# VectorE takes the next piece of scores ahead of a block's low half in two attention stages

## The chip, the cores and the metric

The kernel runs on one core of a Trainium2 chip, as one launch. The time is device microseconds of a run; three runs of the kernel before give a median of 3399.77 us (3396.58 to 3401.65).

The engines named here: TensorE (PE in the profile, PEld its weight loads), VectorE (DVE), ScalarE (ACT), GpSimd (POOL) and SyncE (SP, which issues DMAs). Each executes its own list of instructions in order, and they wait for each other through semaphores.

## The reference

The program computes two transformer layers on 2048 tokens of width 1024, batch 1, float32.

The first layer has two attentions beside each other. The first ("mla") has 8 heads with queries and keys of 96 values and values of 64, causal, with softmax over all earlier keys:

```python
sc = einsum('bqhd,bkhd->bhqk', qb, k) * scale
p = softmax(where(causal, sc, -inf))
o = einsum('bhqk,bkhd->bqhd', p, v)
```

The second ("dsa") has 8 query heads of 64 values that share 2 heads of keys and values. An index score chooses at most 256 earlier keys for each query, and the softmax runs over these alone. Both outputs are gated, projected, weighed with sigmoids, added and projected again. The second layer is a causal window attention of 128 keys with a bias by distance and sink terms, gated and projected, with a norm at the end. The change touches only the two softmax attentions of the first layer.

## The kernel before

The program is a sequence of stages with a barrier after each: front projections, the mla attention, the index scores with the choice of keys (and the gates' projections), the dsa attention, merge, window attention, final. `stage_attention` (line 906) builds both attention stages from a description of the layer (`Mla`, line 1151, and `Dsa`, line 1717).

**Units.** A stage works through 32 units, numbered 0 to 31. A unit has four rows s of 128 queries each, and a number of key blocks j of 128 keys. In mla a unit is one head and 512 queries; its rows see 128(4g+1) to 128(4g+4) keys, and g runs 0, 1, 2, 3, 3, 2, 1, 0 over the units, again and again. Its last four blocks are the diagonal ones, so block 4g+3 concerns only one row (128 columns). In dsa a unit is one tile t of 128 queries and one of the two key heads; its rows are four query heads, all with 128(t+1) keys. The units are t = 0, 0, 1, 1, ... 15, 15. The choice of keys comes as an additive mask.

**Steps.** `schedule` (line 859) writes one list of steps, which every engine walks, each taking its own part:
- "S": one piece of scores, at most 512 keys of one row. TensorE multiplies (three matmuls in mla, two in dsa) into one of 3 PSUM banks `p_s`. VectorE waits for `scored`, adds the mask into `probs` and takes the maximum of the piece (L1051), and increments `moved`. After a row's last piece it reduces the maxima (L1069) and writes the shift (L1073).
- "E": ScalarE takes exp of the row (L1116), after the shift.
- "B": one key block of a unit. TensorE transposes the exps of up to four rows into one of 3 banks `p_t` (L1021). ScalarE copies it, rounded, to `th`, the high half (L1124, `hi_done`). VectorE subtracts and writes the rest to `tl`, the low half (L1081, `lo_done`). Three blocks later TensorE multiplies both with the values into `p_o` (L985, L987).
- "V": TensorE transposes the inverted sums (L1033), ScalarE copies them (L1131). VectorE has no part in it; it inverts the sums at the unit's block 0 (L1089).
- "O": VectorE multiplies the output with them (L1102).

**The order.** The unit with "S" steps is one ahead of the unit with "B" steps. Each unit begins with a lead of 8 "S" (or all, where there are fewer), then the blocks of the unit before follow, and the rest of the "S" is spread evenly between them. Written with S for a piece, S. for the last piece of a row, e for its exp, B for block 0, b for a later block, the list of unit 28 of mla and that of unit 12 of dsa (with the blocks of units 27 and 11) are

```
SSSS.SeSSS.BSebbOSbbSbbS.bbSebbSbbSbbS.bVe
SS.SeS.SeS.SeS.BbbObbVe
```

**What waits for what.** Before the scores of piece i TensorE waits until piece i-3 is moved (line 1012), before the transposes of a block until the low three uses of `p_t` earlier is done (`wait_bank`, line 995). VectorE waits for `scored` (line 1050) before a piece and for `hi_done` (line 1080) before a low. ScalarE writes a slot of `th` only after the multiplication four blocks earlier.

Of the kernel before, what the change touches and what calls it, by code (L numbers as in the profile page):

```python
# [858 lines left out]
def schedule(units, behind, lead, output_late, batched):  # L859

    steps, late = [], []
    blocks = 0
    for n in range(len(units) + behind):
        m = n - behind
        s_steps = []
        if n < len(units):
            for s in range(4):  # L870
                keys = units[n]["keys"][s]
                for c, k0 in enumerate(range(0, keys, GT)):
                    s_steps.append(("S", n, s, c, k0, min(GT, keys - k0), k0 + GT >= keys))
        b_steps = [("B", m, i, j, s0) for i, (j, s0) in enumerate(units[m]["blocks"])] + [("V", m)] if m >= 0 else []
        pending = []

        def take_scores():
            nonlocal pending
            step = s_steps.pop(0)
            steps.append(step)  # L880
            steps.extend(pending)
            pending = []
            if step[6] and not batched:
                pending = [("E", n, step[2])]
            elif step[6] and step[2] == 3:
                pending = [("E", n, s) for s in range(4)]

        for _ in range(min(lead, len(s_steps))):
            take_scores()
        total, rest = len(b_steps), len(s_steps)  # L890
        for x in range(total):
            steps.append(b_steps[x])
            blocks += steps[-1][0] == "B"
            while late and late[0][1] <= blocks:
                steps.append(("O", late.pop(0)[0]))
            while s_steps and (rest - len(s_steps)) * total < (x + 1) * rest:
                take_scores()
        while s_steps:
            take_scores()
        steps += pending  # L900
        if m >= 0:
            late.append((m, blocks + output_late))
    return steps + [("O", n) for n, _ in late]


def stage_attention(nc, sem, tag, ident, layer, space):


# [3 lines left out]
    R, S = layer.depth, layer.split_ring  # L912
    steps = schedule(units, R - 1, layer.lead, layer.output_late,
                     layer.batched)
    n_b = [sum(len(u["blocks"]) for u in units[:n]) for n in range(len(units) + 1)]
    A = layer.score_banks
    B = 6 - A
    ring = lambda n, place: (n_b[n] + n + place) % B
    n_sub = lambda n, s: 4 * n + s
    with ExitStack() as c:  # L920
# [27 lines left out]
        @block.sync  # L948
        def _(sp):
            ahead = layer.ahead  # L950
            for n in range(ahead):
                layer.load(sp, n)
            for n in range(len(units)):
                if n + ahead < len(units):
                    layer.load(sp, n + ahead)
                if n >= 1:
                    sp.wait_ge(out_done, n)
                    sp.dma_start(layer.store(n - 1), ot[:, (n - 1) % 2]).then_inc(stored[(n - 1) % 2], 16)
                layer.sync_unit(sp, n)
            n = len(units) - 1  # L960
            sp.wait_ge(out_done, n + 1)
            sp.dma_start(layer.store(n), ot[:, n % 2]).then_inc(stored[n % 2], 16)
            for p in range(2):
                sp.wait_ge(stored[p], 16 * len(range(p, len(units), 2)))
            layer.sync_end(sp)
# [73 lines left out]
        @block.vector  # L1039
        def _(dve):  # L1040
            layer.dve_start(dve)
            i = 0
            for step in steps:
                if step[0] == "S":
                    _, n, s, ch, k0, w, last = step
                    if ch == 0:
                        layer.wait_bias(dve, n, s)
                        if n >= R and s == 0:
                            dve.wait_ge(turned, n_b[n - R + 1])
                    dve.wait_ge(scored, i + 1)  # L1050
                    nc.vector.tensor_tensor_reduce(  # L1051
                        out=probs[n % R][:, s, k0:k0 + w], in0=p_s[:, i % A, 0:w],
                        in1=layer.bias(n, s, k0, w), scale=1.0, scalar=layer.least_max(n, s),
                        op0=ALU.add, op1=ALU.max, accum_out=maxes[:, n % R, s, ch:ch + 1]).then_inc(moved, 1)
                    i += 1
                    if layer.batched:
                        if s == 3:
                            if n >= R:
                                dve.wait_ge(exped, n_sub(n - R, 3) + 1)
                            dve.wait_ge(moved, i)  # L1060
                            nc.vector.tensor_scalar(shift[:, n % R], maxes[:, n % R, :, 0], -layer.scale, None,
                                                    ALU.mult).then_inc(shifted, 1)
                            layer.shift_made(dve, n, shift[:, n % R])
                    elif last:
                        m = maxes[:, n % R, s, 0:1]
                        dve.wait_ge(moved, i)
                        if ch > 0:
                            m = top[:, n % R, s:s + 1]
                            nc.vector.tensor_reduce(m, maxes[:, n % R, s, 0:ch + 1], AX.X, ALU.max)  # L1069
                            dve.drain()  # L1070
                        if n >= R:
                            dve.wait_ge(exped, n_sub(n - R, s) + 1)
                        nc.vector.tensor_scalar(shift[:, n % R, s:s + 1], m, -layer.scale, None,  # L1073
                                                ALU.mult).then_inc(shifted, 1)
                elif step[0] == "B":
                    _, n, place, j, s0 = step
                    b = n_b[n] + place
                    if b >= S:
                        dve.wait_ge(multiplied, b - S + 1)
                    dve.wait_ge(hi_done, b + 1)  # L1080
                    nc.vector.tensor_tensor(tl[:, b % S, s0 * P:GT], p_t[:, ring(n, place), s0 * P:GT],  # L1081
                                            th[:, b % S, s0 * P:GT].bitcast(F32),
                                            ALU.subtract).then_inc(lo_done, 1)
                    if place == 0:
                        dve.wait_ge(exped, n_sub(n, 3) + 1)
                        layer.add_sinks(dve, n, sums[:, n % R])
                        if n >= 2:
                            dve.wait_ge(inv_turned, n - 1)
                        nc.vector.reciprocal(inv[:, n % 2], sums[:, n % R]).then_inc(inverted, 1)  # L1089
                elif step[0] == "O":  # L1090
                    n = step[1]
                    dve.wait_ge(multiplied, n_b[n + 1])
                    dve.wait_ge(spread_done, n + 1)
                    if not layer.packed:
                        if n >= 2:
                            dve.wait_ge(stored[n % 2], 16 * (n // 2))
                        nc.vector.tensor_tensor(ot[:, n % 2], p_o[0:HD, n % 2], spread[0:HD, n % 2],
                                                ALU.mult).then_inc(out_done, 1)
                        continue
                    if n >= 2:  # L1100
                        dve.wait_ge(out_done, n - 1)
                    nc.vector.tensor_tensor(halves[:, n % 2], p_o[:, n % 2], spread[:, n % 2],  # L1102
                                            ALU.mult).then_inc(weighed, 1)
# [1874 lines left out]
def program(nc, a, out):  # L2978
    with ExitStack() as c:
# [16 lines left out]
        with ExitStack() as c1:  # L2996
            bias = BiasJob(nc, c1, a["one_hot"], a["t5_table_2"], spread)
            at, end = -(-nc.sbuf_base // 64) * 64, nc.sbuf_usable_end
            rest = Space(nc, (at + 2 * H_HALF, end))
            index_in = IndexInputs(nc, rest, at, qiT, kiT, wi, h_dram, a["w_in"][0],  # L3000
                                   a["b_merge"][0].rearrange("a n -> (a n)"))
            kept = rest.ranges[0][0]
            mla = Mla(nc, qkT, va, oaT, bias, at, kept)
            mla.index_in = index_in
            stage_front(nc, sem, ident, a, h_dram, qkT, qbT, kbT, qiT, kiT, va, vb, wi, bias, mla)
            sem.end_stage()
            stage_attention(nc, sem, "mla", ident, mla, Space(nc, (kept + H_HALF // 4, end)))
            sem.end_stage()
# [72 lines left out]
```

## Time and profile before

| | |
|---|---|
| median of three runs | 3399.77 us |
| profiled execution, its own time | 3407.41 us |
| its span | 3405.6 us |
| granted TensorE clock, mean | 0.965 |
| TensorE busy | 3153.2 us (93%) |
| VectorE busy | 2075.5 us (61%) |
| ScalarE busy | 1823.7 us (54%) |
| mla attention | about 447.6 to 938.7 us of the span |
| dsa attention | about 1617.2 to 2082.1 us |

"Busy" counts from the start of an instruction to its end; instructions of one engine can overlap in the profile, so two that follow without a gap are often less than one duration apart. An idle time in brackets in a timeline is the time before that instruction in which its engine did nothing, and the name behind the arrow is what ended it.

### The profile page before, as it was taken

How to read it: one execution, taken by the hardware profiler on the slowest of the kernel's cores; microseconds unless marked ns; L12 is line 12 of the kernel's file. 1: busy time of each engine (PE TensorE's matmuls, PEld its weight loads, DVE VectorE, ACT ScalarE, POOL GpSimd, SP SyncE). 2: the span in 40 equal slices, each digit the busy share in tenths (PEclk: the TensorE clock that was granted, in tenths of full speed). 3: DMA queues.
4: the chain of work that ended last, by engine and by line, in shares of the span. 5: the costliest groups of instructions: out<-in, count | busy, mean ns of one | idle time of the engine just before them, and what ended most of it. 6: DMA issues, size and time to landing. Idle time of an engine off the chain costs nothing. (4 is left out here: it accounts for less than half of the span.)

```text
span 3405.6 us, 51222 instructions
## 1 busy us (share of the span) xinstructions
PE 3153.2 (93%) x17304; PEld 2648.2 (78%) x17304; DVE 2075.5 (61%) x5122; ACT 1823.7 (54%) x3613; POOL 779.4 (23%) x1078
## 2 busy tenths in 40 slices
PE   6999879999979999996899997899989999969998
PEld 5888768888868777775667776899878888859997
DVE  5767668888845756663899885444446666632112
ACT  5665556667656666663777774211246666632121
POOL 6444411111112122232211101111034444311110
PEclk8999989999989999998899998999999999979999
DMA  4666654436152222235411103444432222144432
GB/s 166 203 199 199 204 132 97 88 69 141 58 196 85 67 88 77 79 91 124 107 42 31 31 19 110 147 133 138 165 135 74 74 65 64 55 143 133 124 124 74
DMA packets 307189, 370.46 MB, mean 109 GB/s; under 512 B 24801, under 2 KB 251937, under 8 KB 303089
## 3 DMA queue, kind: packets, MB, share of 16 engines
q1 hardware_dynamic: 293728, 320.77, 32.5%
q0 software_dynamic: 13200, 46.42, 4.3%
q8 instruction: 139, 2.28, 0.3%
q14 instruction: 122, 0.99, 0.1%
HBM read 216.32 MB, written 150.80 MB: 108 GB/s over the span
## 5 line engine op out<-in xcount | busy, mean ns | idle before, releaser
L93 PE MATMUL i_p_g<-i_hT_lo,i_wh 128*128 128x512 f32 x768 | 308.9, 402 | 9.3 <-DVE i_wl L1632 9.3
L94 PE MATMUL i_p_g<-i_hT_hi,i_wl 128*128 128x512 f32 x768 | 306.7, 399 | 0.0
L95 PE MATMUL i_p_g<-i_hT_hi,i_wh 128*128 128x512 f32 x768 | 306.2, 399 | 0.0
L1650 DVE SCALAR_TENSOR_TENSOR i_score<-i_relu,i_w,i_score 128x1024 f32<-128x1024 f32 (+7 forms) x154 | 155.1, 1024 | 167.9 <-ACT i_relu L1534 166.1
L1544 ACT ACTIVATE i_above<-i_score,i_less 128x2048 bf16<-128x2048 f32 (+13 forms) x140 | 183.2, 1308 | 105.7 <-POOL i_less L1601 69.1
L1081 DVE TENSOR_TENSOR mla_tl<-mla_p_t,mla_th 128x512 fp32r<-128x512 f32 (+1 forms) x320 | 186.2, 606 | 45.2 <-ACT mla_th L1124 41.9
L1124 ACT ACTIVATE mla_th<-mla_p_t 128x512 fp32r<-128x512 f32 (+1 forms) x320 | 164.0, 530 | 86.9 <-PE mla_p_t L1021 84.1
L1081 DVE TENSOR_TENSOR dsa_tl<-dsa_p_t,dsa_th 128x512 fp32r<-128x512 f32 x272 | 180.1, 686 | 42.8 <-ACT dsa_th L1124 37.1
L1051 DVE CUSTOM_DVE_ANT_0 dsa_probs<-dsa_p_s,dsa_mask 128x512 f32<-128x512 f32 (+3 forms) x320 | 184.6, 605 | 26.4 <-PE dsa_p_s L1796 24.7
L1124 ACT ACTIVATE dsa_th<-dsa_p_t 128x512 fp32r<-128x512 f32 x272 | 155.4, 593 | 70.5 <-PE dsa_p_t L1021 69.5
L1534 ACT ACTIVATE i_relu<-i_p_s 128x1024 f32<-128x1024 f32 (+7 forms) x176 | 141.5, 813 | 77.2 <-PE i_p_s L1502 38.6
L1021 PE MATMUL mla_p_t<-ident,mla_probs 128*128 128x128 f32 x1088 | 172.7, 274 | 10.9 <-DVE mla_tl L1081 9.5
L93 PEld LDWEIGHTS i_p_g<-i_hT_lo,i_wh 128*128 128x128 f32 x768 | 146.3, 191 | 45.2 <-issue 10.2
L1116 ACT ACTIVATE dsa_probs<-dsa_probs,dsa_shift 128x128 f32<-128x128 f32 (+15 forms) x128 | 153.9, 1202 | 43.7 <-DVE dsa_shift L1073 43.3
L93 PE MATMUL b_p_p<-b_wl,b_xh 128*128 128x512 f32 (+1 forms) x384 | 161.8, 421 | 14.9 <-DVE b_wl L588 14.9
L1116 ACT ACTIVATE mla_probs<-mla_probs,mla_shift 128x1280 f32<-128x1280 f32 (+15 forms) x128 | 153.6, 1201 | 40.5 <-DVE mla_shift L1073 39.0
L1021 PE MATMUL dsa_p_t<-ident,dsa_probs 128*128 128x128 f32 x1088 | 169.8, 280 | 5.9 <-ACT dsa_probs L1116 2.7
L1795 PE MATMUL dsa_p_s<-dsa_k_hi,dsa_q 128*128 128x512 f32 (+3 forms) x320 | 131.6, 413 | 45.9 <-PEq L70 25.6
L95 PEld LDWEIGHTS i_p_g<-i_hT_hi,i_wh 128*128 128x128 f32 x768 | 146.3, 190 | 35.4
L93 PE MATMUL m_p_b<-m_ol,m_bh 128*128 128x256 f32 x512 | 148.9, 291 | 26.6 <-POOL m_ol L2690 22.3
L1021 PEld LDWEIGHTS dsa_p_t<-ident,dsa_probs 128*128 128x128 f32 x1088 | 134.1, 143 | 50.1 <-DVE dsa_tl L1081 19.7
L94 PEld LDWEIGHTS i_p_g<-i_hT_hi,i_wl 128*128 128x128 f32 x768 | 146.4, 191 | 31.4
(334 smaller groups left out, 9699.4 us busy)
## 6 DMA issues: line engine op xcount, KB each, us to landing
scratch_gates<-i_ob SPq DMA_DIRECT2D x96, 256.0 KB, 2.4
m_m<-scratch_gates SPq DMA_DIRECT2D x64, 256.0 KB, 4.2
f_hs<-scratch_h2T SPq DMA_DIRECT2D x16, 1024.0 KB, 9.8
scratch_qkT<-b_th SPq DMA_DIRECT2D x64, 192.0 KB, 2.6
scratch_qkT<-b_tl SPq DMA_DIRECT2D x64, 192.0 KB, 2.9
i_ws<-in_w_in SPq DMA_DIRECT2D x24, 512.0 KB, 4.6
b_xt<-in_x SPq DMA_DIRECT2D x16, 512.0 KB, 4.9
scratch_h<-b_xh POOLq DMA_DIRECT2D x16, 512.0 KB, 3.0
```

Of the source, the lines that this page charges most:

```text
L93: pe.matmul(out, l[0], r[1], start=start, stop=False)
L94: pe.matmul(out, l[1], r[0], start=False, stop=False)
L95: return pe.matmul(out, l[0], r[0], start=False, stop=stop)
L1021: last = nc.tensor.transpose(p_t[:, ring(n, place), s * P:(s + 1) * P], probs[n % R][:, s, j * P:(j + 1) * P], ident[:])
L1051: nc.vector.tensor_tensor_reduce(out=probs[n % R][:, s, k0:k0 + w], in0=p_s[:, i % A, 0:w], in1=layer.bias(n, s, k0, w), scale=1.0, scalar ...
L1081: nc.vector.tensor_tensor(tl[:, b % S, s0 * P:GT], p_t[:, ring(n, place), s0 * P:GT], th[:, b % S, s0 * P:GT].bitcast(F32), ALU.subtract). ...
L1116: nc.scalar.activation(x, x, ACT.Exp, bias=shift[:, n % R, s:s + 1], scale=layer.scale, accum_out=sums[:, n % R, s:s + 1]).then_inc(exped, 1)
L1124: nc.scalar.activation(th[:, b % S, s0 * P:GT], p_t[:, ring(n, place), s0 * P:GT], ACT.Copy).then_inc(hi_done, 1)
L1534: nc.scalar.activation(relu[:, n % 3, 0:width], p_s[:, n % 2, 0:width], ACT.Relu).then_inc(relued, 1)
L1544: nc.scalar.activation(above[:, 0:keys], score[:, x % 2, 0:keys], ACT.Sign, bias=less[:, x % 2:x % 2 + 1], accum_out=signs[:, i % 2:i % 2 ...
L1650: nc.vector.scalar_tensor_tensor(out=acc, in0=r, scalar=w[:, t, h:h + 1], in1=acc, op0=ALU.mult, op1=ALU.add).then_inc(summed, 1)
L1795: self.nc.tensor.matmul(out, q, self.k_hi[:, g, k0:k0 + w], start=True, stop=False)
```

## The change

VectorE walks a reordered copy of the step list in both attention stages. `scores_ahead` holds back each "B" step except a unit's block 0 until the next "S" has been taken, or until another "B" or an "O" comes. "V" and "E" steps, which VectorE skips, are left out of its list and don't end the holding. The other engines walk the list as before.

```diff
@@ -903,6 +903,24 @@
     return steps + [("O", n) for n, _ in late]
 
 
+def scores_ahead(steps):
+
+
+    order, held = [], []
+    for step in steps:
+        if step[0] == "S":
+            order += [step] + held
+            held = []
+        elif step[0] in "BO":
+            order += held
+            held = [step] if step[0] == "B" and step[2] else []
+            if step[0] == "B" and not step[2]:
+                order.append(step)
+            if step[0] == "O":
+                order.append(step)
+    return order + held
+
+
 def stage_attention(nc, sem, tag, ident, layer, space):
@@ -1040,7 +1058,7 @@
         def _(dve):
             layer.dve_start(dve)
             i = 0
-            for step in steps:
+            for step in scores_ahead(steps):
                 if step[0] == "S":
                     _, n, s, ch, k0, w, last = step
                     if ch == 0:
```

## Rows read from the trace of the kernel before

**Rows 1.** Windows: busy us (and instructions) by engine, clock, DMA, in each stage.
```profile
447.60:938.70 491.10, 476.47 (x2816) 398.18 (x2816) 408.55 (x1247) 339.72 (x609) 58.66 (x64) 0.98 0.42 96
1617.20:2082.10 464.90, 432.89 (x2400) 331.00 (x2400) 403.96 (x1199) 332.23 (x561) 58.58 (x62) 0.97 0.18 43
```
**Rows 2.** Groups by shape, VectorE, mla: xcount | busy, mean ns | idle before, releasers.
```profile
L1081 DVE TENSOR_TENSOR mla_tl<-mla_p_t,mla_th 128x512 fp32r<-128x512 f32 x224 | 148.5, 686 | 43.7 <-ACT mla_th L1124 41.9 <-issue 0.6
...
L1081 DVE TENSOR_TENSOR mla_tl<-mla_p_t,mla_th 128x128 fp32r<-128x128 f32 x32 | 9.2, 286 | 0.3
```
**Rows 3.** Waits in the dsa stage: who <- whom: us in total, times, longest us.
```profile
PEld dsa_p_s L1795 <- DVE dsa_maxes L1051: 58.7, 115, 1.3
ACT dsa_probs L1116 <- DVE dsa_shift L1073: 43.3, 74, 1.2
DVE dsa_tl L1081 <- ACT dsa_th L1124: 37.1, 62, 3.7
...
PEld dsa_p_t L1021 <- DVE dsa_tl L1081: 19.7, 46, 1.0
```
**Rows 4.** Timeline, dsa unit 12: start us, us, instruction [idle before <-releaser].
```profile
1702.21 0.69 DVE L1081 TENSOR_TENSOR dsa_tl<-dsa_p_t,dsa_th 128x512 fp32r<-128x512 f32 x1 [0.21 <-ACT dsa_th L1124]
...
1702.45 0.39 PE L1796 MATMUL dsa_p_s<-dsa_k_lo,dsa_q 128*128 128x512 f32 x1
...
1703.02 0.69 DVE L1051 CUSTOM_DVE_ANT_0 dsa_probs<-dsa_p_s,dsa_mask 128x512 f32<-128x512 f32 x1
...
1703.63 0.56 DVE L1051 CUSTOM_DVE_ANT_0 dsa_probs<-dsa_p_s,dsa_mask 128x384 f32<-128x384 f32 x1
...
1704.25 0.19 PEld L1795 LDWEIGHTS dsa_p_s<-dsa_k_hi,dsa_q 128*128 128x128 f32 x1 [0.18 <-DVE dsa_maxes L1051]
```
**Rows 5.** Timeline, start of dsa unit 22.
```profile
1845.96 0.39 PE L1796 MATMUL dsa_p_s<-dsa_k_lo,dsa_q 128*128 128x512 f32 x1
...
1846.60 0.68 DVE L1051 CUSTOM_DVE_ANT_0 dsa_probs<-dsa_p_s,dsa_mask 128x512 f32<-128x512 f32 x1
```
**Rows 6.** Timeline, end of dsa unit 29, start of unit 30.
```profile
2011.17 0.34 PE L1796 MATMUL dsa_p_s<-dsa_k_lo,dsa_q 128*128 128x384 f32 x1
...
2012.03 0.55 DVE L1051 CUSTOM_DVE_ANT_0 dsa_probs<-dsa_p_s,dsa_mask 128x384 f32<-128x384 f32 x1
...
2013.03 0.69 DVE L1051 CUSTOM_DVE_ANT_0 dsa_probs<-dsa_p_s,dsa_mask 128x512 f32<-128x512 f32 x1
```
**Rows 7.** Timeline, start of mla unit 14.
```profile
668.29 0.39 PE L95 MATMUL mla_p_s<-mla_k_hi,mla_q_hi 96*128 96x512 f32 x1
...
668.83 0.69 DVE L1051 CUSTOM_DVE_ANT_0 mla_probs<-mla_p_s,mla_none 128x512 f32<-128x512 f32 x1 [1.02 <-PE mla_p_s L95]
...
669.58 0.19 PEld L93 LDWEIGHTS mla_p_s<-mla_k_lo,mla_q_hi 96*128 96x128 f32 x1 [0.31 <-DVE mla_maxes L1051]
```
**Rows 8.** Timeline of ScalarE, mla unit 15.
```profile
686.26 0.60 ACT L1116 ACTIVATE mla_probs<-mla_probs,mla_shift 128x384 f32<-128x384 f32 x1
```
**Rows 9.** Timeline, mla unit 13, blocks 12 to 15 of unit 12.
```profile
664.73 0.39 PE L95 MATMUL mla_p_s<-mla_k_hi,mla_q_hi 96*128 96x512 f32 x1
...
665.66 0.68 DVE L1051 CUSTOM_DVE_ANT_0 mla_probs<-mla_p_s,mla_causal 128x512 f32<-128x512 f32 x1
...
666.43 0.27 PE L1021 MATMUL mla_p_t<-ident,mla_probs 128*128 128x128 f32 x1
...
666.73 0.89 DVE L1081 TENSOR_TENSOR mla_tl<-mla_p_t,mla_th 128x384 fp32r<-128x384 f32 x2
```
**Rows 10.** Timeline of weight loads, dsa unit 21.
```profile
1839.86 0.44 PEld L1021 LDWEIGHTS dsa_p_t<-ident,dsa_probs 128*128 128x128 f32 x4 [0.20 <-DVE dsa_tl L1081]
```
**Rows 11.** Timeline, dsa unit 28, blocks 1 and 5 of unit 27.
```profile
1975.22 0.69 DVE L1081 TENSOR_TENSOR dsa_tl<-dsa_p_t,dsa_th 128x512 fp32r<-128x512 f32 x1 [1.29 <-ACT dsa_th L1124]
...
1977.18 0.42 PEld L1021 LDWEIGHTS dsa_p_t<-ident,dsa_probs 128*128 128x128 f32 x4 [0.52 <-DVE dsa_tl L1081]
```

## The prediction

> **What bounds the kernel now.** I read the slice table of the page first, then the busy time of the two attention stages, the waits inside each, and last the timeline of each engine where the new order differs. Both stages are TensorE's: it is busy 476.5 of 491.1 us in the first and 432.9 of 464.9 us in the second [rows 1]. VectorE has 408.6 and 404.0 us of work there, 83% and 87% [rows 1], and is never far from the path, because TensorE runs at most three banks ahead of it on either kind of work. VectorE idles 41.9 us in the first stage before lows, until ScalarE has written the high half [rows 2], and 37.1 us in the second, at 62 places [rows 3]. In the second stage TensorE's weight loads wait 58.7 us for a score bank and 19.7 us, at 46 places, for a low [rows 3]. The reader is to see that VectorE has idle time, and to ask whether it lies where order can use it.
>
> **What the edit does to the order.** Worked out from the step list, it exchanges 98 neighbouring pairs (low, piece of scores) in the first stage and 90 in the second. It adds and removes no instruction, no DMA and no semaphore; all other engines keep their lists. VectorE executes in order, so what moves is a wait: at such a pair it waits for `scored` first, and the low stands behind that wait. Who waits for a low: TensorE, three blocks later. Who waits for a piece: TensorE, three pieces later, and at a row's end ScalarE's exp.
>
> TensorE issues a block's transposes, two multiplications of an older block, then the piece, and ScalarE's copy takes less time than those matmuls. If nobody is behind, the old order is thus the order in which things become ready, and the new one can only win where ScalarE is late with the high half.
>
> **Unit starts, second stage (+9.3).** A "V" step does not release a held low, so the last low of a unit also goes behind the first piece of the next lead. Unit 12: the low runs at 1702.21 while TensorE still computes the piece, whose last matmul ends at 1702.45 + 0.39 = 1702.84; VectorE starts it at 1703.02 (0.18 us after) and the next at 1703.63, so a step costs 0.61 us start to start [rows 4]. New: VectorE idles to 1703.02, takes the piece to 1703.63 and the low to 1704.24; the second piece is 0.61 us late. The lead of eight pieces runs at VectorE's pace: TensorE's load of the fifth waits 0.18 us for the bank of the second [rows 4], so it moves too, and so do the exps, which wait 43.3 us of the stage for shifts [rows 3]. Nothing later in the unit gives this back, since the whole chain moves. Alike are units 10 to 16 and 24: 8 x 0.61 = 4.9 us. In units 8 and 9 VectorE reached the piece a little late, 0.45 each by the same arithmetic, 0.9. Unit 5 has one piece a row, and its exps may cover it: I take 0. In units 17 to 23 VectorE was just behind: in unit 22 the piece's last matmul ends at 1845.96 + 0.39 = 1846.35, so it was ready at 1846.53, and VectorE, in the low until then, took it at 1846.60 [rows 5]. That low began 0.61 us before, at 1845.99. New: idle to 1846.53, pair done at 1847.75 instead of 1847.21, 0.54 late. Seven such, at 0.5: 3.5. Bounds of the term: 0, and 18 x 0.61 = 11.0.
>
> **Unit ends, second stage (+2.0).** In units 25 to 31 the last pair is a low and the short last piece. In unit 29 its second matmul ends at 2011.17 + 0.34 = 2011.51, ready about 2011.69; piece, maximum and shift take 2013.03 - 2012.03 = 1.00 us [rows 6]; with the low behind it, the next unit starts at 2013.30, 0.27 late. The seven give 0.1 to 0.4 each, 2.0 us (bounds 0 and 3).
>
> **First stage (+9.2).** A unit's last low has 128 columns and takes 0.29 us, its end hidden under the next instruction [rows 2], 0.28 start to start. At 668.83 VectorE had waited 1.02 us for the first piece, so the low was free; behind the piece it makes the second 0.28 us late, and TensorE waits for banks here also, 0.31 us at 669.58 [rows 7]. 23 of the units 2 to 31 have more than one piece a row: 6.4 us. Seven have one, and there the exps follow each other without a gap (one at 686.26 with no wait before it) [rows 8], so ScalarE hides the delay; without that cover it would be 7 x 0.28 = 2.0, and I take 0. Bounds 0 and 8.4.
> One inner pair hurts more, in units 5, 13, 21 and 29: the low of block 12 goes behind a row's last piece and its shift. The piece is ready at 664.73 + 0.39 + 0.15 = 665.27 (0.15 as between 668.29 + 0.39 and 668.83 [rows 7]) and takes 666.73 - 665.66 = 1.07 us with its shift; the low then ends at 666.34 + 0.69 = 667.03. TensorE took block 15, which needs that low, at 666.43 [rows 9], and goes on 0.6 to 0.7 us later; the unit's end and the next lead hang on it. 4 x 0.7 = 2.8 us, bounds 0 and 3. The other inner pairs of this stage fall where VectorE is behind anyway or idles next: 0.
>
> **Inner pairs, second stage (-1.1).** Loss: in units 21 to 23 TensorE already waits for the low of block 3 (0.20 us at 1839.86 [rows 10]), which now comes 0.61 later; I count 0.4 each, 1.2 us (0 to 1.8). Gain: in units 24 to 28 VectorE idles 1.1 to 1.3 us before the low of block 1, because ScalarE is in an exp, and the piece behind it is long computed. It now fits into that wait: the low stays at 1975.22, what follows comes 0.61 earlier, and TensorE's wait of 0.52 us at 1977.18 goes [rows 11]. Late next is the high half, so not all of it counts: 5 x 0.45 = 2.3 us (0 to 3.1).
>
> A rule of the Trainium skill, page "Perfetto Trace Analysis", section "Identifying the Most-Contended Engine", is to optimise the engine of highest occupancy first (for TensorE it wants other measures than matmul time). TensorE's busy share is 97% and 93% [rows 1], so by that rule a new order of equal work on VectorE would leave 3400 us. The bank waits of [rows 4, 7] speak against it at unit starts.
>
> **Sum.** 9.3 + 2.0 + 9.2 - 1.1 = 19.4 us slower. The profiled execution took 3407.4 us (span 3405.6), 7.6 above the runs' median of 3399.8; the sum gives 3427 against itself and, carried over, 3419 for the median. Nothing outside the two stages changes.
>
> **Rivals.**
> A. Faster: the piece fills ScalarE's exp waits, the 79 us of [rows 2, 3]. But they must fall on exchanged pairs. Following the timeline, 44 of the 188 pairs have one, 17 us in all, mostly of the size in [rows 4] (0.21); nine are of 0.8 us or more, like that of [rows 11]. If these nine gave 0.6 each and ScalarE covered every unit start, 3399.8 - 5.4 = 3394. It decides from the point where the exps set the pace of a lead; the 43.3 us that ScalarE waits for shifts [rows 3] say that VectorE does. Chance 0.07.
> B. Same: three banks absorb 0.3 to 0.6 us at a unit start, and what is left cancels, 3400 (3393 to 3407). For it: the occupancies [rows 1]. Against: TensorE waits for banks at just these places [rows 4, 7], so the ring is used up there. Chance 0.13.
> C. Slower by more: lows that come 0.61 us or, behind a shift, about 1 us later lengthen the 46 waits for lows of [rows 3]. At 0.2 us each that is 9 us on top: 3428. Against: most of these waits follow a late high half, which the order doesn't move. Chance 0.12.
> D. As summed, perhaps with part of a term hidden: 3410 to 3425. Chance 0.68.
> That the list is not what it seems (a pair not exchanged) would show as B.
>
> 0.2% (6.8 us) is about what a measurement of this kernel can tell from no change. Faster by more: A, 0.07. Within: B, 0.13. Slower: C and D, 0.80. The range takes in D, most of C and the half of B nearest to it: 3398 to 3431.
>
> **What would show it.** In the changed profile the first stage is about 9 us longer and the second about 10. VectorE's waits for `scored` appear at nearly every unit start of the second stage, while its waits for the high half shrink by at most some 10 us a stage. TensorE's waits for score banks in the leads grow, block 15 of units 5, 13, 21 and 29 waits for a low, and the wait of 0.52 us before block 5 in unit 28 is gone. I am wrong if those waits of VectorE appear and the stages keep their length (the ring absorbs them), or if TensorE's waits for banks and lows fall in sum.

## Result and the profile after

Five runs of each: 3416.02 us median (3415.96 to 3417.91) against 3399.77 us (3396.58 to 3402.76). The ratio is 1.0050, 95% interval 1.0040 to 1.0061: slower by 16.3 us by the medians. The profiled execution has a span of 3416.1 us, against 3405.6.

The windows of the two stages in the changed kernel, which answer to [rows 1] (stretch, length, busy us of PE, PEld, DVE, ACT, POOL, clock, DMA share, GB/s):

```profile
446.80:944.90 498.10, 480.27 (x2816) 398.17 (x2816) 409.55 (x1248) 339.52 (x609) 58.57 (x64) 0.98 0.42 94
1622.60:2095.00 472.40, 430.95 (x2400) 329.73 (x2400) 405.41 (x1199) 330.91 (x561) 58.44 (x62) 0.98 0.18 42
```

The first stage is 7.0 us longer (498.1 - 491.1), the second 7.5 (472.4 - 464.9). VectorE's work is the same to 1.5 us. TensorE's busy time is 3.8 us more in the first stage and 1.9 less in the second; its idle time grew by 3.2 and 9.4 us. Between the whole spans of these two profiled executions lie only 10.5 us (3416.1 - 3405.6), because the stages whose code did not change took 4.0 us less in the second of them. The profile before also holds an accident that can be placed: its granted clock was below full speed for part of a 20 us stretch of the second stage, and the two units there (8 and 9) took 10.26 and 11.05 us, where the profiles of inner pairs alone and of block 1 alone (below) show 8.65 and 9.46. The same stretch in the windows of the kernel before and of the changed kernel:

```profile
1660.00:1680.00 20.00, 17.84 (x86) 13.36 (x85) 15.73 (x61) 12.56 (x26) 3.75 (x4) 0.83 0.31 61
```
```profile
1660.00:1680.00 20.00, 16.64 (x91) 11.64 (x89) 17.55 (x62) 14.07 (x31) 5.64 (x6) 1.00 0.28 57
```

The clock was 0.83 in the first and 1.00 in the second. Put right by 1.6 + 1.6 us, the second stage grew by 10.7.

Waits in the second stage after, as in [rows 3] (who <- whom: us in total, times, longest us):

```profile
PEld dsa_p_s L1813 <- DVE dsa_maxes L1069: 66.2, 112, 1.3
ACT dsa_probs L1134 <- DVE dsa_shift L1091: 52.5, 66, 1.6
DVE dsa_probs L1069 <- PE dsa_p_s L1814: 42.4, 36, 21.9
DVE dsa_tl L1099 <- ACT dsa_th L1142: 27.8, 48, 3.0
...
PEld dsa_p_t L1039 <- DVE dsa_tl L1099: 18.6, 41, 1.0
```

The wait of VectorE for pieces in the kernel before:

```profile
DVE dsa_probs L1051 <- PE dsa_p_s L1796: 24.7, 3, 21.8
```

VectorE's wait for the high half fell from 37.1 to 27.8 us. In its place stands a wait for pieces, 36 times instead of 3; the longest, 21.8 us before and 21.9 after, is the start of the stage, so the rest grew from 2.9 to 20.5 us. Behind it TensorE waits longer for banks (58.7 to 66.2) and ScalarE for shifts (43.3 to 52.5). In the first stage the same trade, groups by shape as in [rows 2]; the last line is that of the kernel before for the same pieces:

```profile
L1099 DVE TENSOR_TENSOR mla_tl<-mla_p_t,mla_th 128x512 fp32r<-128x512 f32 x224 | 148.9, 686 | 31.2 <-ACT mla_th L1142 28.9 <-issue 0.6
L1069 DVE CUSTOM_DVE_ANT_0 mla_probs<-mla_p_s,mla_none 128x512 f32<-128x512 f32 x192 | 129.0, 687 | 27.8 <-PE mla_p_s L95 27.2
...
L1051 DVE CUSTOM_DVE_ANT_0 mla_probs<-mla_p_s,mla_none 128x512 f32<-128x512 f32 x192 | 127.8, 686 | 16.1 <-PE mla_p_s L95 15.4
```

The wait for the high half fell from 41.9 to 28.9 us, that for these pieces rose from 15.4 to 27.2.

**A unit start, second stage.** Unit 12 after, the timeline of VectorE and of the weight loads, to be laid beside [rows 4]:

```profile
1708.51 0.69 DVE L1069 CUSTOM_DVE_ANT_0 dsa_probs<-dsa_p_s,dsa_mask 128x512 f32<-128x512 f32 x1 [1.01 <-PE dsa_p_s L1814]
...
1709.13 0.69 DVE L1099 TENSOR_TENSOR dsa_tl<-dsa_p_t,dsa_th 128x512 fp32r<-128x512 f32 x1
1709.73 0.55 DVE L1069 CUSTOM_DVE_ANT_0 dsa_probs<-dsa_p_s,dsa_mask 128x384 f32<-128x384 f32 x1
...
1710.34 0.19 PEld L1813 LDWEIGHTS dsa_p_s<-dsa_k_hi,dsa_q 128*128 128x128 f32 x1 [0.78 <-DVE dsa_maxes L1069]
```

The low, which ran in a gap before, waits through 1.01 us of idle VectorE, and the second piece starts 1.22 us after the first instead of 0.61. The load of the fifth piece, which waited 0.18 us, waits 0.78 (the last line shown). (Unit 11 has six blocks, so the list of unit 12 ends in `BbbObbbVe`, with one b more behind the O than shown ahead; the pair at the unit start is the same.)

**Inside a unit, first stage.** Unit 13 after, to be laid beside [rows 7, 9]:

```profile
667.57 0.69 DVE L1069 CUSTOM_DVE_ANT_0 mla_probs<-mla_p_s,mla_causal 128x512 f32<-128x512 f32 x1 [0.67 <-PE mla_p_s L95]
...
668.64 1.49 DVE L1099 TENSOR_TENSOR mla_tl<-mla_p_t,mla_th 128x512 fp32r<-128x512 f32 x3
671.47 0.69 DVE L1069 CUSTOM_DVE_ANT_0 mla_probs<-mla_p_s,mla_none 128x512 f32<-128x512 f32 x1 [1.35 <-PE mla_p_s L95]
...
672.09 0.28 DVE L1099 TENSOR_TENSOR mla_tl<-mla_p_t,mla_th 128x128 fp32r<-128x128 f32 x1
672.29 0.28 DVE L1069 CUSTOM_DVE_ANT_0 mla_probs<-mla_p_s,mla_causal 128x128 f32<-128x128 f32 x1
...
669.39 0.14 PEld L1039 LDWEIGHTS mla_p_t<-ident,mla_probs 128*128 128x128 f32 x1 [0.81 <-DVE mla_tl L1099]
```

The row's last piece and its shift go first, the low of block 12 only at 668.64, and TensorE waits 0.81 us for it before block 15. At the start of unit 14 VectorE's wait for the first piece grew from 1.02 to 1.35 us, and the low, free before, stands between the first and the second piece.

**The gain.** Unit 28 after, to be laid beside [rows 11]:

```profile
1986.83 0.69 DVE L1069 CUSTOM_DVE_ANT_0 dsa_probs<-dsa_p_s,dsa_mask 128x512 f32<-128x512 f32 x1
...
1988.11 1.29 DVE L1099 TENSOR_TENSOR dsa_tl<-dsa_p_t,dsa_th 128x512 fp32r<-128x512 f32 x2 [0.58 <-ACT dsa_th L1142]
```

The wait for the high half shrank from 1.29 to 0.58 us, because the piece fits into it, and two lows follow each other without a gap. TensorE's wait of 0.52 us before block 5 is gone; at the load behind that one a wait of 0.35 us for a low is new, so not all of it is gained.

### The profile page after: what moved, and what is told of

Same layout as the page of the kernel before. It is cut to its first block and busy times, and to the rows that moved or that the text cites. A ratio compares the mean times of both kernels' runs of the same rounds, so it can differ in the third digit from the quotient of the medians.

```text
span 3416.1 us, 51222 instructions
## 1 busy us (share of the span) xinstructions
PE 3152.4 (92%) x17304; PEld 2644.2 (77%) x17304; DVE 2077.7 (61%) x5122; ACT 1821.2 (53%) x3613; POOL 777.6 (23%) x1078
## 5 line engine op out<-in xcount | busy, mean ns | idle before, releaser
L1099 DVE TENSOR_TENSOR mla_tl<-mla_p_t,mla_th 128x512 fp32r<-128x512 f32 (+1 forms) x320 | 186.5, 605 | 32.6 <-ACT mla_th L1142 28.9
L1099 DVE TENSOR_TENSOR dsa_tl<-dsa_p_t,dsa_th 128x512 fp32r<-128x512 f32 x272 | 179.6, 685 | 31.4 <-ACT dsa_th L1142 27.8
L1134 ACT ACTIVATE dsa_probs<-dsa_probs,dsa_shift 128x128 f32<-128x128 f32 (+15 forms) x128 | 153.8, 1201 | 53.0 <-DVE dsa_shift L1091 52.5
L1039 PEld LDWEIGHTS mla_p_t<-ident,mla_probs 128*128 128x128 f32 x1088 | 133.4, 140 | 50.9 <-DVE mla_tl L1099 21.0
L1039 PEld LDWEIGHTS dsa_p_t<-ident,dsa_probs 128*128 128x128 f32 x1088 | 132.7, 142 | 49.3 <-DVE dsa_tl L1099 18.6
```

The source lines that it names most:

```text
L1039: last = nc.tensor.transpose(p_t[:, ring(n, place), s * P:(s + 1) * P], probs[n % R][:, s, j * P:(j + 1) * P], ident[:])
L1134: nc.scalar.activation(x, x, ACT.Exp, bias=shift[:, n % R, s:s + 1], scale=layer.scale, accum_out=sums[:, n % R, s:s + 1]).then_inc(exped, 1)
```

## Experiments

To place a difference I take from each timeline the moment at which VectorE starts a unit's first piece; the time to the next unit's first piece is the unit's length. Away from the first units of a stage (up to unit 7 in the second) and from disturbed clock, equal code gives equal lengths to 0.04 us, which makes them sharper than the time of a run. One length falls out: unit 26 of the second stage is 0.35 us longer in wait alone, at full granted clock and without an exchanged start, and I have not traced why. Lengths in us:

```
unit                  mla 5   mla 9  mla 13  dsa 12  dsa 21  dsa 25  dsa 30
before                22.17    8.83   22.51   11.29   17.46   20.52   24.06
changed               22.93    9.03   22.95   11.88   18.58   20.08   24.24
starts alone          22.35    9.02   22.67   11.89   18.00   20.52   24.05
inner pairs alone     22.74    8.83   22.75   11.29   18.18   20.08   24.23
block 1 alone         22.15    8.83   22.50   11.29   17.47   20.13   24.05
late V                21.88    8.47   22.12   11.08   17.46   20.51   24.05
changed + late V      22.50    8.59   22.70   11.46   18.16   20.06   24.25
wait alone            22.34    9.01   22.34   11.85   17.94   20.53   24.05
```

Sums of lengths run, if nothing else is said, to the start of unit 31, in the first stage from unit 2 and in the second from unit 5, since no low is exchanged in the units ahead of these. (Those units differ from profile to profile all the same: unit 2 of the second stage is 0.65 us longer in the changed kernel and in inner pairs alone.) Units 8 and 9 of the second stage are compared with those of block 1 alone, because the profile before is disturbed there. Summed in this way the change costs 6.1 us in the first stage and 10.1 in the second, 16.2 us, against 16.3 by the medians.

The diffs show the lines that decide; `late_turn` and `follows_v` are helpers that move the V steps and find the exchanged starts.

**Starts alone.** The exchanges across a V step, no others.

```diff
-            held = [step] if step[0] == "B" and step[2] else []
+            held = [step] if step[0] == "B" and step[2] and steps[x + 1][0] == "V" else []
```

> Only the exchanges across a V step are made (26 in the first stage, 18 in the second): the last low of a unit goes behind the first piece of the next. Readiness theory (at a unit start VectorE idles until the first piece is computed, and the low then delays the second piece): 0.2 us at each start of the first stage, about 4.5 to 5 us, and 0.5 to 0.6 us at each start of the second, about 9.5 us; 3399.8 + 14 = 3414, most of the change's 16 us. Rival (the lows inside the units, which TensorE waits for, carry the loss): at most 4 us, 3404.

3415.86 us against 3401.22 for the kernel before on that chip, ratio 1.0040 (1.0027 to 1.0053). The lengths: 0.2 us in 22 units of the first stage, 4.3 in sum from unit 2 on; 0.42 to 0.62 at each start of the second, 10.0 in sum. For unit 8, disturbed in this profile too (10.29 us), that sum takes the 0.51 us of the changed kernel, which makes the same exchange there. So most of the loss is here.

**Inner pairs alone.** V releases a held low.

```diff
-        elif step[0] in "BO":
+        elif step[0] in "BOV":
             order += held
```

> Only the exchanges inside a unit are made (72 and 72); a V step releases a held low. Readiness theory: units 5, 13, 21, 29 of the first stage +0.25 to 0.55 each (block 15 waits for the low of block 12), 1.6 to 2 us; second stage +0.5 in units 21 to 23, -0.45 in units 24 to 28 and the last-piece pairs of units 25 to 31 a further 1 to 2, so 0 to +1.5; in all +2 to +4, 3403. Rival (inner lows carry the loss): +12 or more, 3412.

3403.83 us, ratio 1.0006 (0.9997 to 1.0015), no change by time. The lengths show what cancels: first stage +0.57 and +0.24 in units 5 and 13, as in 21 and 29, with small ones 2.1 in sum; second stage +0.7 to +0.9 in units 21 to 23 and -0.3 to -0.6 in 24 to 28, +0.5 in sum. By time the rival of this expectation, 12 us or more for the inner lows, is out. In unit 21 the weight load that waited 0.20 us for the low [rows 10] waits 0.61 more:

```profile
1836.74 0.20 PEld L1036 LDWEIGHTS dsa_p_t<-ident,dsa_probs 128*128 128x128 f32 x2 [0.81 <-DVE dsa_tl L1096]
```

Starts and inner pairs together are 4.3 + 2.1 and 10.0 + 0.5, 16.9 us, against 16.2 for the whole change by the same sums; unit by unit they add, to 0.25 us or better (in dsa 21, 0.54 + 0.72 against 1.12).

**Block 1 alone.** The nine pairs where VectorE idled 0.8 to 1.3 us.

```diff
-            held = [step] if step[0] == "B" and step[2] else []
+            held = [step] if step[0] == "B" and step[2] == 1 else []
```

(V releases here too.)

> Only the nine exchanges of a block 1 with the piece behind it are made (units 3, 11, 19, 27 of the first stage, units 24 to 28 of the second), where VectorE idles 0.8 to 1.3 us for the high half. Readiness theory: the piece fits in the wait; second stage -0.3 to -0.5 us in each of its five units, first stage nothing since TensorE does not wait there; -2 us, 3398, at the edge of what timing can tell, but to be seen in the units' lengths. Rival (the high half is late next, the gain is given back within the unit): lengths unchanged to 0.1 us.

3398.05 us, ratio 0.9989 (0.9981 to 0.9998). Units 24 to 28 of the second stage are 0.57, 0.39, 0.62, 0.55 and 0.60 us shorter, 2.7 in sum; the four of the first stage are unchanged to 0.05. The order of the change is right at these five places.

**Late V.** The kernel before, with each V step moved behind the first piece of the next unit, on all engines.

```diff
-    steps = schedule(units, R - 1, layer.lead, layer.output_late,
-                     layer.batched)
+    steps = late_turn(schedule(units, R - 1, layer.lead, layer.output_late,
+                     layer.batched), 1)
```

> The kernel before (no exchange on VectorE), with every V step moved behind the first piece of the next unit on all engines, so that TensorE computes that piece 0.36 us earlier. If the wait of VectorE for the first piece of a unit sets the lead's pace: first stage, where VectorE waits 0.4 to 1.0 us at most starts, up to 0.3 us at each of 26 starts, 4 to 8 us less; second stage, where it waits only 0.12 us at nine starts, about 1 us less; 3391 to 3395. Rival (TensorE's own work is the bound and the place of the V makes no difference): 3400 within 2 us.

3389.43 us, ratio 0.9966 (0.9954 to 0.9978). In the first stage, units 14 and 15 are 0.35 and 0.53 us shorter, 7.1 in all from unit 1 to the end of the stage (5.6 by the sums used above). VectorE's wait before the first piece of unit 14, 1.02 us in [rows 7], is 0.21:

```profile
669.94 0.69 DVE L1070 CUSTOM_DVE_ANT_0 mla_probs<-mla_p_s,mla_none 128x512 f32<-128x512 f32 x1 [0.21 <-PE mla_p_s L95]
```

In the second stage units 9 to 15 and 23 gain 0.2 each, and unit 1 gains 1.9, which I had not foreseen: the expected 3391 to 3395 does not hold it. The first piece of a unit is thus on the path, by an experiment that does not touch the lows.

**The change with late V.** Both edits.

> The changed kernel with every V step moved behind the first piece of the next unit. Readiness theory: the first piece is computed 0.3 us earlier, so an exchange at a start of the second stage costs 0.4 to 0.45 us against the kernel with late V alone, where it cost 0.6 without late V; in the first stage VectorE idles before the piece either way, so the small low still costs 0.2. Sum against late V alone +13 to +15, 3403 to 3405. Rival (the cost of an exchange is fixed, 0.6, whatever the readiness): +17, 3407, and 0.6 at each start of the second stage.

3398.19 us against 3402.93 for the kernel before on that chip, ratio 0.9990 (0.9981 to 0.9999). This expectation missed: against late V alone the lengths grow by 3.4 us in the first stage and by 3.9 in the second (here from unit 0, as its units 4 to 7 differ between these two profiles by more than the exchanges make), not by 13 to 15. The direction was right and the size was not. At the start of unit 12 the wait for the piece is 0.58 us and no longer 1.01:

```profile
1690.43 0.69 DVE L1088 CUSTOM_DVE_ANT_0 dsa_probs<-dsa_p_s,dsa_mask 128x512 f32<-128x512 f32 x1 [0.58 <-PE dsa_p_s L1833]
...
1691.04 0.69 DVE L1118 TENSOR_TENSOR dsa_tl<-dsa_p_t,dsa_th 128x512 fp32r<-128x512 f32 x1
```

An exchange there costs 11.46 - 11.08 = 0.38 us instead of 11.88 - 11.29 = 0.59, and in units 17 to 20, where VectorE was a little behind, 0.10 to 0.20 instead of 0.53 to 0.62. An earlier piece makes the exchange cheaper, as the readiness theory has it and a fixed cost has not. In the first stage the lengths say where the cost fell from 6.1 to 3.4 us: units 5, 13, 21 and 29, with the pair at block 12, still carry 2.4, units 3, 11, 19 and 27 another 0.9, and all others together 0.1, so the low at a unit start has become almost free. In unit 14 the third piece starts 1.25 us after the first in the kernel before and 1.45 in the changed one; with late V it is 1.36 and 1.45. That fits with V, which TensorE now computes between the first and the second piece, making the later pieces late by itself, so that part of the low falls into that time; no run isolates it.

**Wait alone.** The order of the kernel before; at the 44 starts the low also waits for the piece.

```diff
                     dve.wait_ge(hi_done, b + 1)
+                    if place and place == len(units[n]["blocks"]) - 1 and follows_v(steps, x):
+                        dve.wait_ge(scored, i + 1)
```

> The order of the kernel before, but at the 44 unit starts where the change exchanges a low and a first piece the low also waits until that piece is computed; then the low, then the piece. Wait theory (the loss is VectorE's idle time before a piece that isn't ready, not which of the two goes first): units as long as with the exchanges at unit starts alone, second stage +0.55 to 0.6 at each, first +0.2 to 0.3, 3413 to 3416. Rival (the order matters, since the second piece is what is late): 3401 to 3405.

3412.87 us, ratio 1.0036 (1.0022 to 1.0050) against the kernel before on that chip (3402.93), just below the 3413 to 3416 expected and the loss of starts alone within the intervals. Unit 12:

```profile
1700.89 0.69 DVE L1088 TENSOR_TENSOR dsa_tl<-dsa_p_t,dsa_th 128x512 fp32r<-128x512 f32 x1 [0.98 <-PE dsa_p_s L1803]
1701.50 0.68 DVE L1056 CUSTOM_DVE_ANT_0 dsa_probs<-dsa_p_s,dsa_mask 128x512 f32<-128x512 f32 x1
```

The low is first again, yet idle time of 0.98 us stands before the pair, and the unit takes 11.85 us, as with the exchange (11.88). In the second stage the sum is 9.4 us, without the 0.35 of unit 26, against 10.0 with the exchange. (The low now delays the first piece itself, so the cost begins to count in the unit that ends, 4 and 7 instead of 5 and 8, and the sum is taken from unit 4.) In the first stage the sum is 3.4 us instead of 4.3, and not unit by unit: unit 13 is 0.17 us shorter than in the kernel before. So the order of the two makes little of the loss; that VectorE holds back work it could do makes nearly all of it.

**Late V and block 1.** The two edits that gained, with V behind the first piece and behind the second.

> Late V and only the nine exchanges of block 1. The two gains lie at different places (unit starts; the exp before block 1), so they add: 3389.5 - 2.7 = 3386.5 to 3388. Rival (a gain of one takes the other's away, since the exps now run at other times): 3389.5 to 3390.

> As the last, with V behind the second piece of the next unit. Readiness theory: the first piece was VectorE's only wait; at the second VectorE is busy with the first, so V there only frees ScalarE for the exp a little earlier: 3385 to 3388. Rival (V so late holds back the output and the bank of p_t): 3390 or more.

3385.08 us, ratio 0.9953 (0.9939 to 0.9967), and 3384.91 us, ratio 0.9944 (0.9931 to 0.9958), both a little below what was expected: the gains add, units 24 to 28 of the second stage are shorter by what block 1 alone gave, and by time one place of V is not told from the other. By the lengths, V behind the second piece takes 1.0 us more from the first stage. Both beat the kernel before, by some 16 and 19 us (0.0047 and 0.0056 of 3400), and so the changed one by 32 to 35.

## Why the prediction was right

**The mechanism.** It held as written: a held low waits behind a piece that is not ready. The changed unit starts show it, and the wait alone makes the same loss. The whole was predicted at +19.4 us and measured at +16.3, inside the range. The difference of 3.1 us lies in the first stage (9.2 predicted, 6.1 measured); in the second the net of 10.2 us met 10.1, though its parts were off in both directions.

**Unit starts, second stage.** 9.3 us predicted, 10.0 by the lengths of starts alone. The step of unit 12 (0.61) measured 0.59, but that of unit 16, counted alike, 0.42; those of units 17 to 23 measured 0.51 to 0.62 against 0.5, and those of units 8 and 9 0.51 and 0.60 against 0.45. Unit 5, taken as 0, cost 0.56: its exps did not cover it.

**Unit ends and inner pairs, second stage.** +0.9 net predicted (2.0 + 1.2 - 2.3), +0.5 measured, with two errors that cancel. Units 21 to 23 lost 2.4 us, twice what I counted: in each of them TensorE's wait for the low of block 3 went from 0.20 to 0.81 us, the full 0.61. Of the 0.1 to 0.25 beyond it I can place only a new wait for a low of 0.49 us late in unit 23; unit 20, which has the exchange at a row's last piece but none at block 3, lost 0.12. The ends cost about 0.8, not 2.0: taking inner pairs alone less block 1 alone, unit 29, for which the prediction worked out 0.27, gives 0.08, and unit 30 gives 0.18. The gain was 2.7 against 2.3.

**First stage.** The mis-sized term: 9.2 us predicted, 6.1 measured (7.0 in the profile, of which 0.9 lies in units 0 and 1, which hold no exchanged low). A low of 128 columns delays the next piece by 0.20 us, not 0.28: it starts at 672.09 and the piece at 672.29. And I counted 23 starts where 22 pay, not the same ones: units 4, 12, 20 and 28, at whose start no low is exchanged, cost nothing, and three with one piece a row (8, 16, 24) cost 0.2 each although I had them hidden under exps. 22 x 0.2 = 4.3 instead of 6.4. The pair at block 12 cost 0.57 in units 5 and 21 but 0.24 in units 13 and 29, together 1.6, not 2.8: I had sized all four by one unit.

**The rivals.** A: the exp waits are there, and worth 2.7 us where the piece fits in; the changed kernel has those 2.7 us as well and loses about seven times as much elsewhere (16.3 + 2.7 = 19.0). B: TensorE was 97% and 93% busy by its matmuls, and reordering equal work on VectorE cost 16 us all the same, while moving one step of TensorE gained 12. The prediction set beside B a rule of the Trainium skill, page "Perfetto Trace Analysis", section "Identifying the Most-Contended Engine", and read it by these matmul shares. The section itself says that for TensorE this share is no good measure and names the busy share of the weight loads as one to use instead. In the two stages the weight loads were busy 398.18 of 491.10 us and 331.00 of 464.90 us [rows 1], 81% and 71%, below VectorE's 83% and 87%. So the rule, read as it stands, did not say that an order on VectorE is free, and no share told the 16 us; the bank waits at the unit starts did. C: TensorE's loads waited 18.6 us for lows in the second stage instead of 19.7, so in sum these waits did not lengthen there, though those in units 21 to 23 did; in the first stage the same sum rose from 17.1 to 21.0 us.

## What to carry to other kernels

On an engine that runs its list in order, put work in the order in which it becomes ready, and ask at each exchanged pair what the engine does between the two moments: the cost of a wrong order is about the idle time that it adds (at the start of unit 12 VectorE idles 0.68 us more and the unit grows by 0.59; with late V it is 0.37 and 0.38), and it is paid where the other engines already stand at the end of their ring, here at the start of most units. Average busy shares and total waits do not tell; a waiting time is a store only at the places that the edit reaches. Where the first piece of a stretch is what everybody waits for, move work of the producer that nobody waits for (here V) behind it.

## What the runs showed that I had not expected

Equal code repeats to hundredths of a microsecond: unit 14 of the second stage took 12.70 and 12.69 us in separate profiles, and 13.29 in the two that exchange the pair at its start. So unit lengths resolve effects of about 0.05 us where run times differ by several. The clearest exceptions were short stretches of lower granted clock in the second stage, at units 8 and 9 of the profile before (0.83 over 20 us, 1.6 us a unit) and at unit 8 of starts alone (0.91 over the same 20 us, 1.1 us). Comparing the spans of two single profiles would have given 10.5 us for a change of 16.
